# First norm of a two-block denoiser by feature tile, with the conditions as the stationary operand

## The reference

```python
cond_lat = jax.nn.silu(c)
cond_ctx = jax.nn.silu(c_ctx)[None, :]
m_l = jnp.split(cond_lat @ ada_w[i] + ada_b[i], N_MOD, axis=-1)
m_c = jnp.split(cond_ctx @ ada_w[i] + ada_b[i], N_MOD, axis=-1)
# y = xf * rsqrt(mean(xf * xf) + EPS) * w;  modulate(h) = h * (1 + scale) + shift
x = x + 0.5 * m_l[2] * swiglu(modulate(rms_norm(x, norm1_w), m_l[0], m_l[1]), w1, w3, w2)
ctx = ctx + 0.5 * m_c[2] * swiglu(modulate(rms_norm(ctx, norm1_w), m_c[0], m_c[1]), w1, w3, w2)
# swiglu(h) = (silu(h @ w1) * (h @ w3)) @ w2,  w1 and w3: 1024 x 2816
```

## Time and profile before

| what | value |
| --- | --- |
| median of 3 runs | 2710.91 us (2708.34 to 2711.96) |
| profiled execution, device time | 2710.11 us |
| span in its trace | 2708.3 us |
| mean granted clock of PE | 0.978 |
| PE busy | 2620.7 us of the span |
| DVE / ACT / POOL busy | 1304.5 / 822.8 / 289.2 us |

### The profile page before, as it was taken

The page is one execution under the profiler, slowest core; times in us unless marked ns, Lnnn a source line. Parts: engine busy times, 40 slices in busy tenths (PEclk is TensorE's granted clock), DMA queues, the critical chain, the costliest instruction groups (busy, mean ns, idle before and its releaser), DMA issues.

```text
span 2708.3 us, 30968 instructions
## 1 busy us (share of the span) xinstructions
PE 2620.7 (97%) x12976; PEld 2082.7 (77%) x12976; DVE 1304.5 (48%) x1999; ACT 822.8 (30%) x1212; POOL 289.2 (11%) x226
## 2 busy tenths in 40 slices
PE   7999999999999899999999999999999999999998
PEld 6888888888756775788887776787788678786666
DVE  5565443426345864677657433432332242475563
ACT  3211111124333152322224413122322312245663
POOL 0100000012111540000000011110100011110001
PEclk9999999999999889999999999999999999999999
DMA  7244333312111001354441110110021011011011
GB/s 278 90 144 150 137 128 113 122 62 78 55 37 67 23 24 62 136 186 173 161 159 66 62 47 24 45 72 32 16 78 55 24 63 62 32 64 63 32 34 45
DMA packets 45594, 223.55 MB, mean 83 GB/s; under 512 B 4704, under 2 KB 6928, under 8 KB 31120
## 3 DMA queue, kind: packets, MB, share of 16 engines
q1 hardware_dynamic: 43200, 213.93, 22.1%
q10 hardware_dynamic: 2256, 7.65, 0.8%
HBM read 219.46 MB, written 2.10 MB: 82 GB/s over the span
## 4 chain that ended last, share of the span: by engine, by line
PE 86%; DVE 7%; ACT 4%; issue 2%; POOL 1%; DMA 1%; SPq 0%; POOLq 0%; DVEq 0%; ACTq 0%
PE ps L425 41%; PE ps L422 12%; PE ps L1340 7%; PE ps L400 3%; PE ps L3211 3%; PE ps L2759 3%; PE ps L1063 1%; PE ps L3419 1%; PE ps L451 1%; PE ps L3323 1%; PE ps L2577 1%; PE ps L3443 1%; ACT wh L365 1%; PE ps L703 1%; DVE wl L372 1%
## 5 line engine op out<-in xcount | busy, mean ns | idle before, releaser
L372 DVE TENSOR_TENSOR wl<-stage,wh 128x2048 fp32r<-128x2048 f32 (+2 forms) x158 | 328.4, 2079 | 636.1 <-ACT wh L365 635.9
L425 PE MATMUL ps<-hl,wh 128*128 128x512 f32 x1184 | 470.4, 397 | 0.0
L425 PE MATMUL ps<-hh,wh 128*128 128x512 f32 x1184 | 470.3, 397 | 0.0
L425 PE MATMUL ps<-hh,wl 128*128 128x512 f32 x1184 | 468.4, 396 | 0.0
L365 ACT ACTIVATE wh<-stage 128x2048 fp32r<-128x2048 f32 (+2 forms) x158 | 269.3, 1705 | 530.4 <-PE ps L425 390.2
L425 PEld LDWEIGHTS ps<-hh,wl 128*128 128x128 f32 x1184 | 224.4, 189 | 52.9
L425 PEld LDWEIGHTS ps<-hh,wh 128*128 128x128 f32 x1184 | 224.4, 189 | 51.6 <-issue 1.2
L425 PEld LDWEIGHTS ps<-hl,wh 128*128 128x128 f32 x1184 | 224.5, 190 | 50.5 <-issue 1.2
L422 PE MATMUL ps<-hh,wh 128*128 128x256 f32 x720 | 204.2, 284 | 4.0 <-DVE r_tb L1470 2.8
L623 DVE CUSTOM_DVE_ANT_0 left<-direct,cond_rows,vecs 128x1024 bf16<-128x1024 f32 x168 | 207.0, 1279 | 0.0
L422 PE MATMUL ps<-hh,wl 128*128 128x256 f32 x720 | 204.3, 284 | 0.0
(11 more groups left out here) (564 smaller groups left out, 4712.8 us busy)
## 6 DMA issues: line engine op xcount, KB each, us to landing
stage<-wts SPq DMA_DIRECT2D x108, 1024.0 KB, 4.8
direct<-wts SPq DMA_DIRECT2D x104, 512.0 KB, 4.1
stage<-wts SPq DMA_DIRECT2D x24, 768.0 KB, 4.2
stage<-wts SPq DMA_DIRECT2D x26, 512.0 KB, 3.3
first<-wts SPq DMA_DIRECT2D x16, 512.0 KB, 11.3
cond_rows<-conds ACTq DMA_DIRECT2D x2, 1024.0 KB, 6.8
x<-xin SPq DMA_DIRECT2D x1, 2048.0 KB, 16.4
out<-x SPq DMA_DIRECT2D x4, 512.0 KB, 2.8
```

Of the source, the lines that this page charges most:

```text
L372: dve.tensor_tensor(wl[m % 2][:, 0:w], stage[m % 2][:, 0:w], wh[m % 2][:, 0:w].bitcast(F32), SUB).then_inc(*w_low.up(m))
L425: i = pe.matmul(bank[b[f]][:, :], w[:, k, cols], s[:, k, LAT], start=st, stop=en, skip_group_check=True)
```

## The change

Loads come in another order. `x` and the context are loaded first, in four pieces of two feature tiles each. Then, behind waits of SP for earlier pieces, come the `ada_w` chunks in groups, and weight chunks 0 and 1 ahead of most of them. The conditions for `row_sums` come late, on SP's queue instead of ACT's.

The modulation of feature tiles 0 to 4 is made on PE the other way round: the two conditions are the stationary operand (128 x 2) and a group of `ada_w` columns is moved through (512 columns for tiles 0 and 1, 512 for 2 and 3, 256 for tile 4; `group_pe`, eight products a group). The result is a row pair [2, 512]; ACT copies it to SBUF (`copy_row`), PE turns it (`turn_group_pe`, four small transposes), and DVE adds the bias. Tiles 5 to 7 go by `row_sums`, six chunks as before.

The squares are no longer added on DVE. PE sums them with a 128 x 128 matrix of ones and F32 products of 512 and 256 columns for each tile, which leaves the sum of every token on all partitions; root and reciprocal then work on 128 x 512 and 128 x 256 values (`factor1`). ACT squares the latents, DVE the context.

After that, DVE and ACT go tile by tile (latents and context of one tile together), and PE makes all products of a tile for w1 and w3 together (`first_products_pe`: 24 products a tile), with groups 1 and 2 of `ada_w` between tiles 1 and 2. Because both results of the first pair end together, the silu no longer lies beside w3's products. Chunk 2 is split into two other buffers (`third`) ahead of the second pair's products.

PE ahead of the first product, before: what stands between the last `ada_w` chunks and L400.

```diff
+GROUPS = ((0, 1), (2, 3), (4,))
+BY_ROWS = (5, 6, 7)
...
+    at = 0
+    for g in GROUPS:
+        out.append(("ada_first", 0, 8, at, 256 * len(g), False))
+        at += 256 * len(g)
+    for k in BY_ROWS:
+        ada("ada_w", k, 1)
+        ada("ada_w", 8 + k, 1)
...
+    rows_at = [DIRECT, DIRECT + 4096, DIRECT + 8192, AREA + 40960, AREA + 45056, HREG + 18432]
+    rows_chunk = [at(f"first{i}", [128, 1024], F32, o_) for i, o_ in enumerate(rows_at)]
+    rows_chunk_in = [signal(f"first_in{i}", 16) for i in range(len(rows_at))]
+    third = [area(f"third{i}", [128, 2048], F32R, 18432 * i + 6144) for i in range(2)]
...
+    def split(m):
+        return third if m == 2 else (wh[m % 2], wl[m % 2])
...
+        for j in range(4):
+            sp.dma_start(x[:, 2 * j:2 * j + 2, LAT], xin[:, 2 * j:2 * j + 2, :]).then_inc(*x_in[j].up(0))
+            sp.dma_start(x[:, 2 * j:2 * j + 2, CTX], cin[:, 2 * j:2 * j + 2, :]).then_inc(*c_in[j].up(0))
+        def load_group(i):
+            n = len(group_in[i])
+            for j in range(n):
+                k = slice(8 // n * j, 8 // n * (j + 1))
+                sp.dma_start(group[i][:, k, :], source(i).rearrange("p (k n) -> p k n", k=8)[:, k, :]).then_inc(*group_in[i][j].up(0))
+        def load_rows(i):
+            sp.dma_start(rows_chunk[i][:, :], source(len(GROUPS) + i)).then_inc(*rows_chunk_in[i].up(0))
+        sp.wait_ge(*x_in[1].at(0))
+        load_group(0)
         load_weights(sp, 0)
         load_weights(sp, 1)
...
+        sp.wait_ge(*group_in[0][2].at(0))
+        load_group(1)
+        sp.dma_start(rows_of[:, :, :].rearrange("p s k -> p (s k)"), conds[:, 0:2048]).then_inc(*rows_in.up(1))
+        sp.wait_ge(*stage_in[1].at(1))
+        for i in range(2):
+            load_rows(i)
+        load_group(2)
+        sp.wait_ge(*group_in[1][1].at(0))
+        for i in range(2, len(rows_at)):
+            load_rows(i)
         load_weights(sp, 2)
         load_weights(sp, 3)
+        for d in range(3):
+            sp.wait_ge(*mod.at(1, (5, 13, 6)[d]))
+            load_direct(sp, d)
...
+    def copy_row(act, g):
+        n = 256 * len(GROUPS[g])
+        act.wait_ge(*mv.at("group", g))
+        if g >= 2:
+            act.wait_ge(*row_turned.at(g - 2))
+        act.activation(row1[g % 2][0:2, 0:n], bank[ROW_BANK[g]][0:2, 0:n], ACT.Copy).then_inc(*row_copied.up(g))
...
+        for k in range(8):
+            act.wait_ge(*x_in[k // 2].at(0))
+            if k >= 3:
+                act.wait_ge(*squares_used.at(k - 3))
+            act.activation(sq1[k % 3][:, LAT], x[:, k, LAT], ACT.Square).then_inc(*squared.up(1, k))
+        for c, cols in ((0, LAT), (1, CTX)):
+            act.wait_ge(*rstd.at(1, c, 0))
+            act.activation(factor1[:, cols], factor1[:, cols], ACT.Sqrt).then_inc(*root.up(1, c))
+        copy_row(act, 0)
+        high_part(act, 0)
+        first_high(act, 0)
+        high_part(act, 1)
+        first_high(act, 1)
         condition_rows(act, 1)
...
+        copy_row(act, 1)
+        copy_row(act, 2)
+        for k in range(2, 8):
+            first_high(act, k)
+        high_part(act, 2)
...
+        for k in range(8):
+            dve.wait_ge(*c_in[k // 2].at(0))
+            if k >= 3:
+                dve.wait_ge(*squares_used.at(k - 3))
+            dve.tensor_tensor(sq1[k % 3][:, CTX], x[:, k, CTX], x[:, k, CTX], MUL).then_inc(*squared_context.up(1, k))
+        for c, cols, b, bc in mod1.sides:
+            dve.wait_ge(*(squares_used.at(7) if c else sums_out.at(1, 0)))
+            dve.tensor_scalar(factor1[:, cols], bank[b][:, bc], 1.0 / D, EPS, MUL, ADD).then_inc(*rstd.up(1, c, 0))
+        for c, cols, b, bc in mod1.sides:
+            dve.wait_ge(*root.at(1, c))
+            dve.reciprocal(factor1[:, cols], factor1[:, cols]).then_inc(*rstd.up(1, c))
+        def group_biased(g):
+            k0, n = GROUPS[g][0], len(GROUPS[g])
+            dve.wait_ge(*row_turned.at(g))
+            dve.tensor_tensor(M1first[:, :, k0:k0 + n, :], bank[TURN_BANK[g]][:, 0:4 * n].rearrange("p (a k s) -> p a k s", a=2, k=n),
+                              bias_first[:, :, k0:k0 + n, :], ADD).then_inc(*mod.up(1, "group", g))
+            tile_gains(k0, n)
+        def tile_gains(k0, n):
+            dve.wait_ge(*mod.last())
+            w = V("norm1_w", k0, n).unsqueeze(2).broadcast_to([128, n, 2])
+            dve.scalar_tensor_tensor(G[:, 0, k0:k0 + n, :], M1[:, 8 + k0:8 + k0 + n, :], 1.0, w, ADD, MUL).then_inc(*gains.up(0, k0))
+        def rows_sums(i):
+            k, a = BY_ROWS[i // 2], i % 2
+            c = k + 8 * a
+            dve.wait_ge(*rows_chunk_in[i].at(0))
+            row_sums(dve, rows_chunk[i], M1[:, c, :], bias1[:, 2 * c:2 * c + 2], True, 1, c)
+        def tile(k):
+            f = mod1.f[k % 2]
+            dve.wait_ge(*gains.last())
+            for c, cols, b, bc in mod1.sides:
+                dve.wait_ge(*(h_low.at(1, c, k - 2) if k >= 2 else rstd.at(1, c)))
+                dve.scalar_tensor_tensor(f[:, cols], x[:, k, cols], mod1.g(k, c), factor1[:, cols], MUL, MUL).then_inc(*scaled.up(1, c, k))
+        def tile_low(k):
+            for c, cols, b, bc in mod1.sides:
+                dve.wait_ge(*h_high.at(1, c, k))
+                dve.scalar_tensor_tensor(hl[:, k, cols], mod1.f[k % 2][:, cols], mod1.s(k, c), hh[:, k, cols].bitcast(F32), ADD,
+                                         SUB).then_inc(*h_low.up(1, c, k))
+        group_biased(0)
+        tile(0)
+        low_part(dve, 0)
+        tile_low(0)
+        low_part(dve, 1)
+        tile(1)
+        tile_low(1)
         dve.wait_ge(*cond.at("rows", 1))
...
+        for i in range(3):
+            rows_sums(i)
+        tile_gains(5, 1)
+        group_biased(1)
+        tile(2)
+        tile(3)
+        tile_low(2)
+        tile_low(3)
+        rows_sums(3)
+        group_biased(2)
+        tile(4)
+        tile(5)
+        tile_low(4)
+        tile_low(5)
+        rows_sums(4)
+        rows_sums(5)
+        tile_gains(6, 2)
+        tile(6)
+        tile(7)
+        tile_low(6)
+        tile_low(7)
+        low_part(dve, 2)
...
+    def group_pe(pe, g):
+        n = 256 * len(GROUPS[g])
+        empty(pe, ROW_BANK[g])
+        for k in range(8):
+            j = k * len(group_in[g]) // 8
+            pe.wait_ge(*group_in[g][j].at(0))
+            i = pe.matmul(bank[ROW_BANK[g]][0:2, 0:n], cs1[:, k, :], group[g][:, k, :], start=k == 0, stop=k == 7, skip_group_check=True)
+        i.then_inc(*mv.up("group", g))
+        emptied[ROW_BANK[g]] = row_copied, (g,)
+    def turn_group_pe(pe, g):
+        pe.wait_ge(*row_copied.at(g))
+        empty(pe, TURN_BANK[g])
+        for j in range(2 * len(GROUPS[g])):
+            i = pe.transpose(bank[TURN_BANK[g]][:, 2 * j:2 * j + 2], row1[g % 2][0:2, 128 * j:128 * j + 128], ident[0:2, 0:2])
+        i.then_inc(*row_turned.up(g))
+        emptied[TURN_BANK[g]] = mod, (1, "group", g)
...
+        for k in range(8):
+            pe.wait_ge(*squared.at(1, k))
+            i = pe.matmul(bank[6][:, :], ones, sq1[k % 3][:, LAT], start=k == 0, stop=k == 7, skip_group_check=True)
+            if k == 7:
+                i.then_inc(*sums_out.up(1, 0))
+            pe.wait_ge(*squared_context.at(1, k))
+            pe.matmul(bank[7][:, CTX], ones, sq1[k % 3][:, CTX], start=k == 0, stop=k == 7,
+                      skip_group_check=True).then_inc(*squares_used.up(k))
+        emptied[6] = rstd, (1, 0, 0)
+        emptied[7] = rstd, (1, 1, 0)
         pe.wait_ge(*cond.at(1))
...
+        group_pe(pe, 0)
+        turn_group_pe(pe, 0)
...
+    def first_products_pe(pe):
+        w1, w3 = W_OF["ffn1_w1", 0, 0], W_OF["ffn1_w3", 0, 0]
+        pe.wait_ge(*w_low.at(w1))
+        empty(pe, *range(6))
+        for k in range(8):
+            if k == 2:
+                group_pe(pe, 1)
+                group_pe(pe, 2)
+                turn_group_pe(pe, 1)
+            elif k == 3:
+                turn_group_pe(pe, 2)
+            for c, cols in ((0, LAT), (1, CTX)):
+                pe.wait_ge(*h_low.at(1, c, k))
+                for m, b in ((w1, SETS[0]), (w3, SETS[1])):
+                    if k == 0 and c == 0 and m == w3:
+                        pe.wait_ge(*w_low.at(w3))
+                    _, h, l = parts(m)
+                    for f in range(2):
+                        to = bank[b[2]][:, 256 * f:256 * f + 256] if c else bank[b[f]][:, :]
+                        for a, (w, s) in enumerate(((h, hh), (l, hh), (h, hl))):
+                            i = pe.matmul(to, w[:, k, 128 * f:128 * f + 128], s[:, k, cols], start=k == 0 and a == 0 and not (c and f),
+                                          stop=k == 7 and a == 2, skip_group_check=True)
+                    if k == 7 and c == 1:
+                        i.then_inc(*gemm.up(m, 0))
+                        gemm.also(m, 1)
...
+                joint = n == 1 and p == 0
+                if joint:
+                    first_products_pe(pe)
...
+                if n == 2 or p:
```

(58 more changed lines are left out.)

65 lines of the change are left out of this document (15 added, 50 removed).

## The result

The changed kernel took 2690.31 us (median of four executions, 2686.34 to 2696.32) against 2709.62 us before (four, 2707.55 to 2711.96): 0.9928 of the time, interval 0.9906 to 0.995.

What follows compares the result with a forecast made beforehand. PE was taken as the bound. Eight steps put the start of chunk 2's products at 88.5 us instead of 96.3, so 7.8 less than 2710.1 gave 2702.3, stated as 2702.5; range 2698 to 2709.5.

Steps and rivals of the forecast that it cites:

- P: Theory after the first result: clock falls behind the start vary by execution, whichever kernel runs; the change gives some 10 us.
- step 1: Squares summed on PE: start at 6.9 us when the constants land, end at 19.7, with 2.5 for low clock.
- Step 2: Factors (scaling, roots, reciprocals): 6.8 us in all, done at 26.5, costing nothing while group 0 covers them.
- Step 3: Group 0 on PE: eight products of 512 columns at 0.86, 6.9 us, ending at 26.6.
- Step 5: Tiles 0 and 1 on PE: 4.16 us each plus 2.5 for low clock, from 33.0 to 43.8.
- Step 6: Groups 1 and 2 between tiles 1 and 2: 10.4 us, turning 0.5, then a 3.5 us wait, to 58.2.
- Step 7: Tiles 2 to 7: 25.0 us plus clock fall 1.7, turning 0.5, wait 0.4; the pair ends at 85.8.
- Step 8: Silu ahead of chunk 2's products: 1.9 us wait plus half of a 1.7 us clock fall; they start at 88.5.
- (a): Rival: products with two stationary columns do not hold the clock in groups 0 to 2; 2709.4 us, no change; chance 0.16.
- (b): Rival: clock stays down up to the first fp32r product, squares too; 19.9 us lost, 2722 us; chance 0.05.
- (c): Rival: constants or `x` land as late as before, shifting the start by up to 4.9 us; 2707 us; chance 0.07.
- (d): Rival: late loads or side chunks make PE wait in 96 to 620 us, losing the gain; 2708 to 2711; chance 0.03.

Runs made afterwards that it cites:

- the repetition: The changed kernel run again unchanged, 12 executions: 2697.34 us, ratio 0.9973 to the kernel before.
- the second: The changed kernel run unchanged once more, in the last set, 11 executions: 2696.24 us, ratio 0.9962 to the kernel before.
- the late start: The changed kernel with three transfers, each waited for, ahead of `x`, to start 11 us late: 2710.5 us, ratio 1.002 to the kernel before.
- the three sets of the kernel before: The kernel before, unchanged, in the three sets of follow-up runs: medians 2706.6 (29 executions), 2707.2 (29) and 2707.1 us (22).
- the moving form: The changed kernel with the two conditions as moving operand again, 128 x 128 of the weights loaded, no row copy or turning: 2704.49 us, ratio 0.9983.

## Why the prediction missed

**The spread of executions was not in the range.** The step that failed is "From there each slot is as before", and with it the bound "about 0.2%": I took everything behind 96 us as fixed. The slots do the same work, but the clock differs from one execution to the next. With that the range held only what can vary ahead of the second pair, and the base of the sum was one execution. One kernel's executions spread with a standard deviation of 2 to 5 us (80 of the kernel before: 2695.5 to 2718.7). How much of that is clock shows when each span is multiplied by its mean granted clock, which takes out what the low stretches cost: for the repetition the deviation falls from 2.1 to 1.2 us, for the second from 3.9 to 0.7, for the late start from 4.3 to 0.9, for the three sets of the kernel before from 3.0 to 4.8 down to 1.4 to 2.0. The median of this product is 2638.5 us in the first four executions of the changed kernel and 2638.1 and 2638.4 in the two repetitions: the same work. The product compares executions of one kernel only: before, the clock column reads 1.00 in the first 60 us although the spacing of instructions says half speed, and after only in the first 12.

So the first result takes apart like this. The changed kernel's four executions had mean clocks of 0.980, 0.983, 0.983 and 0.979, the 23 later ones 0.979 on average; 0.9812 less 0.9788, times 2690, is 6.5 us, and its median was 6.5 below the 2696.8 between the later two. The kernel before was 2.8 above its later 2706.8 (the sets with the repetitions), for which only one of the four clocks is on record, 0.978 against 0.980 later. What is left of 19.3 is 10.0, the start. And the 12.2 us between forecast and result are some 2.3 of the start, 6.5 of the clock, and 3.5 by which the kernel before, with 2710.3 in my sum, was taken too high. P has this behind it: repeated executions, a start moved in both kernels, and the same program in both forms of the stage. What stays open is why those four drew so well (two of them are below all 23 later ones). The three later sets ran on three chips and agree; the chip of the first comparison is not on record. Holding the clock up through that stage, which would show it directly, was not tried.

**The start, step by step.** The mechanism was right; a few sizes were off, which add up to 2.3 us. Two sums were off as well: in step 1, 5.8 + 1.3 is 7.1 and not 6.9, and 2702.3 with the 0.8 of the median is 2703.1 and not 2702.5. Neither changes the outcome.
- Step 1: the constants took 6.5 us from issue to landing, 7.78 instead of 6.9, within the bounds. The low clock lasted the 5 us that I took: L835 pairs take 2.07 us at 7.78 and 1.02 at 12.94.
- Step 2: the factors were done at 26.8 (26.5), under group 0. Step 3: 16 instructions, 0.44 each, so products with two stationary columns cost by the columns moved. The wait that I had put at 6.4 us ahead of the first product was 5.7.
- Step 5: the clock came up after 3.3 us, not 5: 0.8 less. Tiles 0 and 1 ended at 43.5 (43.8).
- Step 6 came out within 0.2 us.
- Step 7: 85.1 instead of 85.8; the 0.4 us wait at tile 6 did not come.
- Step 8 was the largest error: the silu held PE for 1.10 us and not 1.9, because w1's last products end ahead of w3's and ACT reads their banks from 84.42 on, and no fall of the clock followed (0.85 less).

**The rivals.** (a), thin products do not hold the clock, and (b), it stays down until fp32r products, are refuted by the L818 rows at 1.00. (c) came true for 0.9 of its 4.9 us. (d) did not come: from the second pair to 785 us PE waits at the same five places as before and as long, 9.5 us in all, and the start's 10 us arrive at the end. I gave (a) 0.16 because L703 spoke for it; the moving form does lose the clock, the stationary form does not, so L703 was the wrong row to carry over and L451 the right one. As the Trainium skill (TensorE: Matmul & The Clock Gate, Part 1) puts it, the gate opens by how busy PE has been; in these traces busy time does not tell the two forms apart, 100% in both, and the clock does.

## What to carry to other kernels

A result a few microseconds wide on a kernel of 2700 needs some ten executions of each side, or the moment in the trace at which the changed part ends; four executions had doubled the gain. Behind a PE that hardly waits, the start's gain arrives whole: forecast that moment, and give the range the spread of the clock as well. When a wait stays after a reorder, read what the waiting chain's third engine has in its queue: moving one small copy brought the second pair forward by 2.3 us.
